# Hybrid layers in fp32: first attention among projection units, packed units, bias by DMA, a share of the output product among second attention's steps

## The reference

```python
x = x + 0.5 * swiglu(rmsnorm(x, ffn1_norm), ...)          # D_FF = 2816
h = rmsnorm(x, mix_norm) @ w_in                           # 3080 columns
(a_q, a_k, a_v, b_q, b_k, b_v, i_q, i_k, i_w, c_q, c_kv, c_kr) = split_columns(h)
o_a = chunk_relpos_attention(a_q, a_k, a_v, a_rel_bias)   # 6 heads of 64, additive bias
o_b = dsa_attention(rope(b_q), rope(b_k), b_v, rope(i_q), rope(i_k), i_w)
      # index scores of 8 heads of 32, top 128 keys of each query, then 5 heads of 64
o_c = mla_attention(rmsnorm(c_q) @ w_uq, rmsnorm(c_kv) @ w_ukv, rope(c_kr))  # 5 heads, 96
x = x + concat([o_a, o_b, o_c]) @ w_out
x = x + 0.5 * swiglu(rmsnorm(x, ffn2_norm), ...)
```

## Time and profile before

| | |
|---|---|
| time, median of 3 | 4381.65 us (4372.96 to 4385.95) |
| the profiled execution | 4383.03 us, span 4381.4 us |
| TensorE busy | 4066.4 us (93%) |
| VectorE busy | 1714.9 us (39%) |
| ScalarE busy | 1505.5 us (34%) |
| GpSimd busy | 369.0 us (8%) |
| mean granted TensorE clock | 0.926 |
| moved by DMA | 316.51 MB, 72 GB/s |

### The profile page before, as it was taken

How to read it: one execution, slowest core, us unless ns; L and a number is a source line. 1 busy time by engine, 2 the same in 40 slices (tenths; PEclk the granted TensorE clock), 3 DMA queues, 4 the chain that set the end, 5 groups by cost and what they waited for, 6 DMA issues and landing times.

```text
span 4381.4 us, 51384 instructions
## 1 busy us (share of the span) xinstructions
PE 4066.4 (93%) x17788; PEld 3216.0 (73%) x17788; DVE 1714.9 (39%) x2847; ACT 1505.5 (34%) x2448; POOL 369.0 (8%) x374
## 2 busy tenths in 40 slices
PE   8999978799999999967899989899999999789999
PEld 6887755588878887745688868787777668567888
DVE  3323565433323323664433234334432223534442
ACT  3222323432223223324332234435534553533331
POOL 1100011101001100011011000000100000100110
PEclk9999976799999999968799979999899999899999
DMA  3333310023323323200023324131112113222332
GB/s 102 96 97 97 82 42 20 1 82 96 96 82 91 96 96 93 76 19 20 29 82 96 96 86 112 39 83 44 39 54 72 39 44 91 58 73 76 96 98 98
DMA packets 495308, 316.51 MB, mean 72 GB/s; under 512 B 10832, under 2 KB 476368, under 8 KB 494640
## 3 DMA queue, kind: packets, MB, share of 16 engines
q1 hardware_dynamic: 490992, 302.86, 23.8%
q0 software_dynamic: 3008, 9.57, 0.7%
q10 hardware_dynamic: 1152, 2.10, 0.1%
HBM read 309.77 MB, written 4.33 MB: 72 GB/s over the span
## 4 chain that ended last, share of the span: by engine, by line
PE 68%; issue 21%; DVE 3%; ACT 3%; POOL 2%; PEld 1%; DVEq 1%; POOLq 0%; PEldq 0%; ACTq 0%
PE bank L214 19%; PE bank L216 19%; PE bank L215 19%; PE bank L256 1%; PE bank L1728 1%; PE bank L1734 1%; PE bank L1748 1%; PE bank L1737 1%; POOL h_lo L299 1%; PE bank L1028 1%; PE bank L1039 0%; PE bank L1030 0%; PE bank L1031 0%; PE bank L1149 0%; PE bank L648 0%
## 5 line engine op out<-in xcount | busy, mean ns | idle before, releaser
L214 PE MATMUL bank<-h_hi,w_hi 128*128 128x512 f32 (+3 forms) x3240 | 1297.9, 401 | 58.6 <-DVE w_lo L206 29.8
L215 PE MATMUL bank<-h_hi,w_lo 128*128 128x512 f32 (+3 forms) x3240 | 1279.0, 395 | 0.0
L216 PE MATMUL bank<-h_lo,w_hi 128*128 128x512 f32 (+3 forms) x3240 | 1277.7, 394 | 0.0
L206 DVE TENSOR_TENSOR w_lo<-w_raw,w_hi 128x1024 fp32r<-128x1024 f32 x571 | 737.7, 1292 | 1189.4 <-ACT w_hi L199 1183.4
L199 ACT ACTIVATE w_hi<-w_raw 128x1024 fp32r<-128x1024 f32 x571 | 598.4, 1049 | 596.4 <-DMA w_raw<-in_ffn_w_down 320.0
L214 PEld LDWEIGHTS bank<-h_hi,w_hi 128*128 128x128 f32 (+3 forms) x3240 | 612.1, 189 | 228.0 <-ACT lru_x L1831 31.0
L216 PEld LDWEIGHTS bank<-h_lo,w_hi 128*128 128x128 f32 (+3 forms) x3240 | 611.2, 189 | 140.5 <-issue 3.8
L215 PEld LDWEIGHTS bank<-h_hi,w_lo 128*128 128x128 f32 (+3 forms) x3240 | 612.5, 189 | 134.0 <-issue 4.6
L214 PE MATMUL bank<-g_hi,w_hi 128*128 (+1 forms) x880 | 342.3, 389 | 0.0
L215 PE MATMUL bank<-g_hi,w_lo 128*128 (+1 forms) x880 | 342.3, 389 | 0.0
L216 PE MATMUL bank<-g_lo,w_hi 128*128 (+1 forms) x880 | 342.3, 389 | 0.0
(11 more groups left out here) (382 smaller groups left out, 4404.1 us busy)
## 6 DMA issues: line engine op xcount, KB each, us to landing
w_raw<-in_w_in SPq DMA_DIRECT2D x161, 512.0 KB, 3.8
w_raw<-in_ffn_w_gate SPq DMA_DIRECT2D x88, 512.0 KB, 3.8
w_raw<-in_ffn_w_up SPq DMA_DIRECT2D x88, 512.0 KB, 3.8
w_raw<-in_ffn_w_down SPq DMA_DIRECT2D x88, 512.0 KB, 3.5
w_raw<-in_w_up SPq DMA_DIRECT2D x44, 512.0 KB, 3.7
w_raw<-in_w_branch SPq DMA_DIRECT2D x32, 512.0 KB, 3.8
w_raw<-in_w_out SPq DMA_DIRECT2D x24, 512.0 KB, 3.8
w_raw<-in_w_down SPq DMA_DIRECT2D x22, 512.0 KB, 3.5
```

The lines of the kernel that those rows point to most:

```text
L206: dve.tensor_tensor(WL[:, slot(c), 0:w], RAW[:, slot(c), 0:w], WH[:, slot(c), 0:w].bitcast(F32), ALU.subtract).then_inc(w_lo, 1)
L214: pe.matmul(bank, wh, xh, start=start, stop=False)
L215: pe.matmul(bank, wl, xh, start=False, stop=False)
L216: return pe.matmul(bank, wh, xl, start=False, stop=stop)
```

## The change

- **Packing.** The host lays the columns of `w_in` out anew in `w_mix`: index key and index weights in one unit, the last of b_q and b_k in one (the scale of the b_q rows then by an extra VectorE operation, and the b_k rows moved to their place by a DMA on GpSimd's queue), the last of b_v and c_kr in one. 28 units become 25. A second item of the same unit is marked `shared` and has no product of its own.
- **Order.** `first_items` (12 units: index, then q, k, v of A) run alone. All 24 index scores go with them, three an item from the fifth on, with four buffers in place of two, and five selection rounds. Then A's 24 steps run woven with `second_items` (13 units: c_q, c_kv, the rest of B, c_kr), with the places of the Fox attention (scores in banks 0 and 1, transposes in 2 and 4, values in 3, products in 5, postings in 6, norms in 7). One or two selection rounds stand in each step, and the rest in the projections of C. `x` is parked in DRAM behind the norm and loaded again behind A's last values.
- **Bias.** The host expands the bias to 128 x 512 for each head; a DMA brings it whole, and VectorE adds the mask only in a block of 64 x 64. The flip matmuls are gone.
- **Second attention.** Copies, low parts and values stand one or two steps later than before (`late`), transposes have three banks, values one.
- **Output.** The three tiles of A are multiplied by their rows of w_out in eight groups of 9 matmuls among the steps of the second attention (`a_output_pe`, `a_output_dve`), from three row units `U_WOA`. The output stage has five tiles left, 15 matmuls a unit.
- The norms of c_q and c_kv write squares into three buffers without waiting for one another. In all attentions ScalarE copies before it splits.

The core of the diff:

```diff
-N_MIX = 28
+N_MIX = 25
+N_FIRST = 12
 U_UQ = U_MIX + N_MIX
 U_UKV = U_UQ + 2
-U_WO = U_UKV + 2
+U_WOA = U_UKV + 2
+U_WO = U_WOA + 3
...
     def norm_act_parts(act, src, n, width, dim, t0, n0, ready, stat_bank, dst=None):
-            act.wait_ge(nm_stat, t0 + max(k + 1, 2))
-            act.activation(SG[:, k % 2, 0:width], src(k), ACT.Square).then_inc(nm_sq, 1)
+            act.wait_ge(nm_stat, t0 + (max(k + 1, 2) if n == KT else 2))
+            act.activation(square_tile(k, n)[:, 0:width], src(k), ACT.Square).then_inc(nm_sq, 1)
...
+    first_items = (
+        [item(0, "rope", IKT[0:32, :], M=32, cos=2, computed=40),
+         item(0, "v", VB[:, :, 320:328], M=8, rows=slice(32, 40), shared=True)]
+        + [item(1 + t, "rope", IQT[:, t, :], scale=32 ** -0.5, cos=2) for t in range(2)]
+        + [item(3 + t, "copy", QA[:, t, :], scale=CHUNK ** -0.5) for t in range(3)]
+        + [item(6 + t, "copy", KA[:, t, :]) for t in range(3)]
+        + [item(9 + t, "v", VA[:, :, t * P:(t + 1) * P]) for t in range(3)])
+    second_items = (
+        [item(t, "copy", CQR[:, t, :]) for t in range(3)]
+        + [item(3 + t, "copy", CKVR[:, t, :]) for t in range(2)]
+        + [item(5 + t, "rope", QB[:, t, :], scale=0.125) for t in range(2)]
+        + [item(7 + t, "rope", KB_[:, t, :]) for t in range(2)]
+        + [item(9, "rope", QB[:, 2, :], scaled_rows=slice(0, 64))]
+        + [item(10 + t, "v", VB[:, :, t * P:(t + 1) * P]) for t in range(2)]
+        + [item(12, "v", VB[:, :, 256:320], M=64, computed=96),
+           item(12, "rope_in_place", KC[64:96, 0, :], M=96, rows=slice(64, 96), cos=2, shared=True)])
...
-    SC_FROM = 8
+    SC_FROM, SC_EACH = 5, 3
...
+            self.copied, self.subtracted, self.used = (TT, TT + 1, 2 * TT + 1) if late else (LAG, LAG, 2 * TT - 1)
+            self.rounds = self.used - TT + 2
...
+    WITH_PROJECTIONS = Places(lambda n, w: B[n % 2][:, 0:w], lambda m, a, b: B[2 + 2 * (m % 2)][:, a:b], 2,
+                              lambda m, w: (GU[:, 0, 0:w], GU[:, 1, 0:w], PROB2[:, 0:w], PROB3[:, 0:w])[m % 4], PT_X)
+    IN_CB = Places(lambda n, w: B[n % 2][:, 0:w], lambda m, a, b: B[(2, 3, 6)[m % 3]][:, a:b], 3,
+                   lambda m, w: (SG[:, 0, 0:w], SG[:, 1, 0:w], TMP[:, 0:w], T[:, 0, 0:w])[m % 4], PT_CB, late=True)
...
+    def bias_dma(pool, l, h):
+        if h >= 2:
+            pool.wait_ge(smax_done, l * N_STEPS + (TT * (h - 1) + 2))
+            pass_wait(pool)
+        pool.dma_start(BM[:, h % 2, :], A["bias"][bass.ds(l * 6 + h, 1)].rearrange("a p s -> (a p) s")
+                       ).then_inc(bm_in[h % 2], 16)
...
+    def a_output_pe(pe, l, q, m):
+        if m == 0:
+            split_ready(pe, q, U_WOA + 2)
+            pe.wait_ge(y_lo, l * 8 + (3 + 2))
+        pe.wait_ge(wa_done, l * KT + (m + 1))
+        for k in range(3):
+            yh, yl = y_tile(k)
+            last = products(pe, B[(5, 7)[m % 2]][:, :], U_WOA + k, slice(m * P, (m + 1) * P), yh, yl, k == 0, k == 2)
+        last.then_inc(wa_mm, 1)
+        if m == KT - 1:
+            pe.drain()
+            pe.sem_inc(w_used, 3)
...
     def mix_sp
+        sp.wait_ge(hv_done, l * HEADS + 7)
+        pass_wait(sp)
+        sp.dma_start(x_flat, dram_x).then_inc(x_back, 16)
+        for k in range(3):
+            load(sp, q, U_WOA + k, RAW[:, slot(U_WOA + k), :], w_out[k * P:(k + 1) * P, :])
...
     def layer_act
+        act.wait_ge(x_parked, l * 16 + 16)
+        woven(A_ROUNDS, len(second_items) + 2,
+              attend_act_parts(act, a_steps, ..., WITH_PROJECTIONS),
+              project_act_parts(act, q, U_MIX + N_FIRST, second_items, ..., hook=second_hook, banks=IN_FIRST))
+        hi(act, q, U_WOA + 2)
+        def out_hook(e, n):
+            if n in OUT_SPLITS:
+                hi(e, q, U_WO + OUT_SPLITS[n])
...
     def layer_dve
+        def first_hook(e, s):
+            score_dve(e, l * N_SC, s)
+            next_round(rounds, 1 if 8 <= s <= 12 else 0)
+        def hook(e, n):
+            if n % TT == 3 and n // TT + 1 < 6:
+                bias_dve(e, l, n // TT + 1)
+            next_round(rounds, 1 + n % 2)
+        def out_hook(e, n):
+            if n in OUT_SPLITS:
+                lo(e, q, U_WO + OUT_SPLITS[n])
+            if n % TT == 3 and n // TT < KT:
+                a_output_dve(e, l, n // TT)
...
     def layer_pool
+        pool.wait_ge(nm_hf, l * N_T + 16)
+        pass_wait(pool)
+        pool.dma_start(dram_x, x_flat).then_inc(x_parked, 16)
...
     def layer_pe
+        def second_hook(e, s):
+            if s == 9:
+                e.wait_ge(nm_hf, l * N_T + 19)
+            next_parts(norms, NORMS_PE, s)
+        pe.wait_ge(y_lo, l * 8 + (3 + 2))
+        def out_hook(e, n):
+            if n % TT == 2 and n // TT < KT:
+                a_output_pe(e, l, q, n // TT)
+        attend_pe(pe, cb_steps, ..., IN_CB, hook=out_hook, banks=1)
```

More of the change, by code:

```diff
@@ L511, in build, with item @@
     y_lo = sem("y_lo")
-    def item(unit, kind, dst, M=P, kt=KT, col=0, stride=P, scale=1.0, rows=None, cos=0, units=1):
+    def item(unit, kind, dst, M=P, kt=KT, col=0, stride=P, scale=1.0, rows=None, cos=0, units=1, computed=None,
+             shared=False, scaled_rows=None):
+        computed = computed or (rows.stop if rows else M)
         def columns(w, c, k):
@@ L563, in alone, with banked @@
         return unit_starts(items, s) and unit_ends(items, s) and items[s]["units"] == 1
+    def banked(items, s):
+        return sum(1 for t in range(s + 1) if not alone(items, t) and not items[t]["shared"])
+    N_M1, N_M2 = banked(first_items, len(first_items) - 1), banked(second_items, len(second_items) - 1)
+    N_MM = N_M1 + N_M2 + banked(c_items, len(c_items) - 1)
     class Banks:
@@ L1000, in attend_dve, with pair_taken, turned_at @@
             pass
+    def pair_taken(m, n):
+        return m // 8 if m >= 0 and m % 8 == 0 and m < n else None
+    def turned_at(m, n, late):
+        if late and m % TT < 2:
+            return [] if m % TT == 0 else [k for k in (m - 1, m) if 0 <= k < n]
+        return [m] if 0 <= m < n else []
     def attend_pe_parts(pe, steps, n0, l0, h0, s0, y0, at, hook=None, banks=2):
-        for n in range(len(steps) + LAG + 1):
+        for n in range(len(steps) + at.rounds):
             if n < len(steps):
@@ L1042, in attend_pe_parts, with attend_act_parts @@
             yield
-    def pair_taken(steps, n):
-        at = n - LAG - 8
-        return at // 8 if at >= 0 and at % 8 == 0 else None
-    def attend_act_parts(act, steps, n0, h0, s0, y_of, jobs, waits, at):
+    def attend_act_parts(act, steps, n0, h0, s0, y_of, jobs, waits, at, hook=None):
         act.drain()
         pairs = len(jobs) // 3
-        for n in range(len(steps) + LAG + 1):
+        for n in range(len(steps) + at.rounds):
+            if hook:
+                hook(act, n)
             if n < len(steps):
@@ L1058, in attend_act_parts @@
                                accum_out=SUM[:, n % 4:n % 4 + 1]).then_inc(exp_done, 1)
+            for m in turned_at(n - at.copied, len(steps), at.late):
+                w = steps[m]["width"]
+                act.wait_ge(tr_done, n0 + (m + 3))
+                if m % TT == 0:
+                    act.wait_ge(hv_done, h0 + (m // TT + 1))
+                act.activation(at.block(0, steps[m]), at.turned(m, 0, w).rearrange("p (k c) -> p k c", c=P), ACT.Copy
+                               ).then_inc(pt_done, 1)
+            pair = pair_taken(n - TT - at.used, len(steps))
+            if pair is not None:
+                act.wait_ge(hv_done, h0 + (2 * pair + 3))
+                for bank, dst_hi, dst_lo in y_of(steps[8 * pair]["group"]):
+                    act.activation(dst_hi, B[bank][:, :], ACT.Copy).then_inc(y_hi, 1)
+            if n < len(steps):
                 pair = n // 8
@@ L1084, in attend_dve_parts @@
         dve.drain()
-        for n in range(len(steps) + LAG + 1):
+        for n in range(len(steps) + at.rounds):
+            for m in turned_at(n - at.subtracted, len(steps), at.late) if at.late else ():
+                w = steps[m]["width"]
+                dve.wait_ge(pt_done, n0 + (m + 3))
+                dve.tensor_tensor(at.block(1, steps[m]), at.turned(m, 0, w).rearrange("p (k c) -> p k c", c=P),
+                                  at.block(0, steps[m]).bitcast(F32), ALU.subtract).then_inc(pl_done, 1)
             if n < len(steps):
@@ L1104, in attend_dve_parts @@
                                   ALU.mult).then_inc(nrm_done, 1)
-            if LAG <= n < len(steps) + LAG:
-                m = n - LAG
+            for m in turned_at(n - at.subtracted, len(steps), at.late) if not at.late else ():
                 w = steps[m]["width"]
@@ L1110, in attend_dve_parts @@
                                   at.block(0, steps[m]).bitcast(F32), ALU.subtract).then_inc(pl_done, 1)
-            pair = pair_taken(steps, n)
+            pair = pair_taken(n - TT - at.used - (1 if at.late else 0), len(steps))
             if pair is not None:
```

(1 more changed line is left out.)

399 lines of the change are left out of this document (203 added, 196 removed).

## The result

The changed kernel takes **4319.72 us** (median of 4, 4313.27 to 4326.08) beside 4382.27 us of the kernel before: a ratio of 0.986, 95% interval 0.9836 to 0.9884. It is 63 us faster where 124 were forecast; the direction and the range (4185 to 4350) hold, the size does not. The profiled execution took 4313.27 us with a span of 4311.6, and went from 4381.4.

The account below looks back on a forecast made before the run. TensorE bounds projections and output, an engine-to-engine chain attention A, VectorE's late low part holds up C/B. Per layer −41 (first projections and A) + 8.5 (C's projections) − 14 (C/B) − 16.3 (output) = −63; two layers −125: 4258 us, range 4185 to 4350.

Parts of the forecast that it names:

- TensorE has 54 + 8 x 2.04 = 70 us at full clock, 100 at today's 0.69, so it fits, barely.: Attention C/B: TensorE's work with eight added products fits the forecast stage of 106 us, down from 120.2.
- coupled rounds: Rival, woven stage of A: product rounds and attention steps add up, +57 us a layer, 4372 us in all; chance 0.13.
- 1 us a head: Attention C/B: ScalarE waits for a head's values to be used before overwriting the first block, 10 us (0 to 20).
- The 74 us of ten heads: Attention C/B: VectorE sets the pace at 7.4 us a head, 9.58 less the 2.2 it stands.
- the 5.5 us of additions: Attention C/B: VectorE's eight additions for the products of A's w_out rows, counted into the 106 us stage.
- the hand-over of 1.0 us a step: Woven stage of A: engine-to-engine gap without VectorE work, 1.0 us in each of 24 steps, added to VectorE's 115.
- 13 x 0.65 and 2: Woven stage of A: VectorE waits 0.65 us for ScalarE's weight copy in 13 items, plus 2 for drains.
- VectorE is later, so it sets the stage: Woven stage of A: VectorE's 150 us plus a 9 us tail gives 159; TensorE needs only 127.
- Fox attention copies before it splits, and has a tail round more: 0: Second block's Fox stage: changed copy order and one more tail round cost nothing, ±5 us.
- My 8 us by the rule: Woven stage: shared-port rule would lengthen VectorE beside eight GpSimd operations, 8 us a layer, 4274 in all; not adopted.
- the slower rival: Both attention stages: granted clock stays at 1.2 GHz, +62 us a layer, 4507 us in all; chance 0.05.
- only the work saved: Rival: woven stage lasts as long as its two parts did; only three units a layer saved, 4350 us; chance 0.10.

Follow-up runs that it names:

- e2: Changed kernel with the eight products of A's w_out rows together ahead of attention C/B's first step, not one a head among the steps: 4319.0 us.
- e10: Changed kernel with the items of attention A's woven stage laid between 29 rounds in place of 26: 4304.38 us, ratio 0.9807 to the kernel before.
- e8: Changed kernel without the 36 selection rounds in attention A's woven stage, masks kept: 4277.43 us, ratio 0.9743 to the kernel before.
- e4: Changed kernel with each product of A behind its step's scores on TensorE in attention C/B, not ahead of them: 4301.89 us, ratio 0.9804.

## Why the prediction was right and wrong

- **Attention C/B, wrong by +25 a layer, 50 of the 62 us missed.** The failing sentence is "TensorE has 54 + 8 x 2.04 = 70 us at full clock, 100 at today's 0.69, so it fits, barely." It asked whether TensorE has room for the product in the stage, not whether there is room at the product's place. A queue runs in order: what stands right behind the values delays the scores of the next step, and so the mask, whatever pauses there are later in the head. Rival "coupled rounds" had this mechanism, but I placed it in A and priced nothing of it in C/B. The wait for the values, "1 us a head", measured 20.2 us in nine (2.2 each), in the head shown at the half clock.

  With the product ahead of the values the stage is 106.5 us, for 106 forecast, but that is luck in part. The 74 us of ten heads rest on 9.58 us a head, and that is the shortest of the nine intervals in the trace of the kernel before: from the head ahead of those two,

```profile
779.49 0.29 DVE L1109 TENSOR_TENSOR cb_turned_lo<-bank,cb_turned_hi 128x128 fp32r<-128x128 f32 x1 [2.14 <-ACT cb_turned_hi L1074]
```

  it is 14.43 us (to 793.92), and the mean of the nine is 11.7. Without products, so without the 5.5 us of additions, the sum would give 101 us, where e2 measured 110.2.
- **Woven stage of A, wrong by +15.** VectorE's work was right, 117.3 for 115, the clock too, 0.82 for about 0.8. The waits that are in the hand-over of 1.0 us a step came to it as well: for low parts 12.2, for scores and transposes 6.9, and 5.7 of short pauses make 24.8, for 24. The term that failed is that VectorE's waits beyond these are 13 x 0.65 and 2: its waits for ScalarE's copies of weights are 11.9, for postings 4.9, for the norms 2.7, and some 7 more go in pauses below 0.15 us. In the tail it waits 4.9, for 9. The last 7 were there to be read: in the steps from which the 1.0 comes, VectorE is busy 45.5 of 67.2 us, that is 2.8 us a step and not 3.2, so a step has 1.4 us without work [the stretch of rows 3]:

```profile
614.29:681.50 67.21, 43.70 (x122) 28.76 (x122) 45.48 (x126) 18.04 (x51) 7.90 (x8) 0.50 0.06 13
```

  e10 shows that some 10 us of the stage hang on how the items are laid, so "VectorE is later, so it sets the stage" was a half truth; by e8 a half to two thirds of the rounds' work was on the path.
- **First projections, wrong by +6.** Twelve more scores and three an item went as said (the next six readings are 7.5 to 8.5 us apart, 8.0 in the mean; the sum's terms give 7.9). The wait for index_q cost about 5.7 in place of 3 (13.7 us between two readings, less 8.0): TensorE stood 2.2 us, and 12 matmuls of the next product ran at the half clock. The way to the first attention step took 8.7 for 4.3, since three scores, two rounds, two copies and the bias stood on VectorE ahead of the first mask, two of the scores at 1.50 us in place of 0.75, beside GpSimd.
- **Projections of C, wrong by −5.** Seven rounds and the rotations fitted into VectorE's idle time better than I gave them credit for: VectorE is busy 29.7 of 39.7 us.
- **Output, right:** the additions lie 3.40 us apart.
- **Second block, wrong by −23.** "Fox attention copies before it splits, and has a tail round more: 0" saw the round and costed it as a tail. That the same number sets where the items fall was in the diff.
- **Parking, bias, packing, right at nothing or as costed.** The store and reload land in 7.3 to 9.8 us, and no engine's wait for them stands in the table of waits of either layer.
- **The port pair.** VectorE operations lengthened in the woven stage of layer one while GpSimd worked are four, 3.4 us in all: two bias additions, a low part of c_q and, by 0.2, one of weights. Two of them, with a low part of c_q at its usual length between:

```profile
606.00 1.70 DVE L282 TENSOR_TENSOR c_q_lo<-c_scaled,c_q_hi 128x512 fp32r<-128x512 f32 x1
...
609.18 0.69 DVE L282 TENSOR_TENSOR c_q_lo<-c_scaled,c_q_hi 128x512 fp32r<-128x512 f32 x1 [0.69 <-ACT c_q_hi L253]
...
618.47 1.30 DVE L1274 TENSOR_TENSOR a_bias<-a_bias,mask 64x64 f32<-64x64 f32 x1
```

  All four have both inputs in SBUF; masks and low parts of probabilities, which read a PSUM bank, were not lengthened. In C/B four normalizations were, of 256 and 384 columns, up to 1.84 us in place of 0.35; they have one input, in SBUF. The Trainium skill's page "SBUF — State Buffer" (the part "Reading the diagram") lets VectorE and GpSimd exclude one another when VectorE's operation has two inputs in SBUF, against a GpSimd operation that reads SBUF, or is in a mode that takes two ports. The trace agrees with the first case in the four of A; that the normalizations are the second is not shown here. My 8 us by the rule counted every GpSimd operation, where only those beside such an instruction cost.

The clock did not stay at 1.2 GHz through both stages, as the slower rival had it: the granted clock was 0.82 and 0.75. The rival "only the work saved" (4350) was passed by 30 us.

## What to carry to other kernels

Independent matmuls laid into a stage bound by waits cost anything from nothing to their full length, by their place in the queue: here they were free *ahead* of the instruction that waits, and cost all of it right behind the one whose end the other engines wait for (e4, behind the scores, lies between). Before a capacity sum is believed, write down for one period which instruction stands behind which, on every engine. And a count that sets how one stream is laid between another is a size to be tuned by itself: here 69 for 68 was worth some 6 to 15 us and 29 for 26 about 15; a product two steps earlier brought 41. Count from the trace, and not by hand, where the items then stand.

## What the runs showed of the hardware

More work can go with a shorter stage and a higher clock: C/B's steps took 110.2 us without products and 106.5 with seven of them, the granted clock going from 0.78 to 0.86.

And a short pause in a full stretch can cost about twice its length. In the first projections TensorE waited 2.2 us for index_q and then had only six narrow score matmuls to make before the next product:

```profile
444.01 0.90 PE L859 MATMUL bank<-index_k,index_q 32*128 32x256 f32 x4 [2.23 <-DVE index_q L800]
...
446.91 0.63 PE L218 MATMUL bank<-h_hi,w_lo 128*128 128x512 f32 x1
447.34 0.63 PE L219 MATMUL bank<-h_lo,w_hi 128*128 128x512 f32 x1
...
452.43 0.39 PE L217 MATMUL bank<-h_hi,w_hi 128*128 128x512 f32 x1
452.66 0.40 PE L218 MATMUL bank<-h_hi,w_lo 128*128 128x512 f32 x1
```

The next twelve matmuls of 512 columns started 0.43 us apart, at 1.2 GHz, and those after them 0.23 apart, at 2.4: 12 x 0.2 = 2.4 us on top of the 2.2. The granted clock shows it by stretches:

```profile
441.80:445.00 3.20, 0.90 (x4) 0.50 (x4) 1.98 (x3) 0.26 (x1) 0.00 (x0) 1.00 0.56 164
445.00:451.80 6.80, 6.62 (x15) 4.82 (x16) 2.73 (x5) 1.73 (x4) 0.00 (x0) 0.50 0.00 0
451.80:454.00 2.20, 2.20 (x11) 1.82 (x10) 0.00 (x0) 0.00 (x0) 0.00 (x0) 0.98 0.00 0
```
